# Down projections of two feed-forward layers as seven block products instead of eight

## The reference

```python
def conv_ffn(h, w_up, conv_w, conv_b, w_down):
    a, v = jnp.split(h @ w_up, 2, axis=-1)
    a = lax.conv_general_dilated(a, ...) + conv_b
    return (jax.nn.silu(a) * v) @ w_down

def swiglu(x, w_gate, w_up, w_down):
    return (jax.nn.silu(x @ w_gate) * (x @ w_up)) @ w_down
...
x = x + g2 * conv_ffn(hffn, ffn_w_up[layer], ..., ffn_w_down[layer])
...
x = x + 0.5 * swiglu(rms_norm(x, ffn1_norm[l]), ffn1_w_gate[l], ffn1_w_up[l], ffn1_w_down[l])
```

## Time and profile before

| | |
|---|---|
| Median of three runs | 2320.53 us |
| Profiled execution, its own time | 2323.76 us |
| Its span in the profile | 2322.5 us |
| TensorE (PE) busy | 2276.6 us, 98% |
| VectorE (DVE) busy | 1630.0 us, 70% |
| ScalarE (ACT) busy | 1049.5 us, 45% |
| GpSimd (POOL) busy | 667.5 us, 29% |
| Granted TensorE clock, mean | 0.996 of full |

### The profile page before, as it was taken

One profiled execution on the slowest core, in us unless ns is written; L12 is line 12 of the kernel. 1 busy time (PEld: TensorE's weight loads), 2 busy tenths in 40 slices (PEclk: granted clock), 3 DMA queues, 4 the chain that ended last, 5 costly groups with the idle time before them and its releaser, 6 DMA issues.

```text
span 2322.5 us, 33905 instructions
## 1 busy us (share of the span) xinstructions
PE 2276.6 (98%) x13709; PEld 1982.2 (85%) x13709; DVE 1630.0 (70%) x2087; ACT 1049.5 (45%) x1515; POOL 667.5 (29%) x587
## 2 busy tenths in 40 slices
PE   7999999999999999999999999999999999999999
PEld 5888977999887877777999888999888777899987
DVE  6655757988786446736988756988555984788844
ACT  4322244555333447834555445444344363544442
POOL 0111532333122028822333010333010771133200
PEclk9999999999999999999999999999999999999999
DMA  8665025776574320015775525676233212677422
GB/s 293 189 199 164 1 91 142 187 182 154 180 229 141 100 67 1 1 55 145 176 179 147 163 91 163 164 183 153 84 106 93 82 37 73 183 179 179 113 91 82
DMA packets 224083, 304.44 MB, mean 131 GB/s; under 512 B 14314, under 2 KB 165415, under 8 KB 223927
## 3 DMA queue, kind: packets, MB, share of 16 engines
q1 hardware_dynamic: 172980, 219.79, 29.3%
q0 software_dynamic: 50640, 82.29, 17.3%
q10 hardware_dynamic: 306, 0.19, 0.0%
HBM read 300.13 MB, written 2.10 MB: 130 GB/s over the span
## 4 chain that ended last, share of the span: by engine, by line
PE 82%; DVE 9%; POOL 3%; issue 2%; ACT 2%; DMA 1%; ACTq 0%; DVEq 0%; POOLq 0%
PE ps L728 45%; PE ps L1133 10%; PE ps L1135 10%; PE ps L1134 10%; DVE w_lo L2245 2%; DVE dsa_mask L2969 1%; POOL hg_k L3269 1%; PE ps L1259 1%; POOL nsa_p L3359 1%; PE ps L1275 1%; DVE small L2967 1%; DMA m_raw<-in_ada_w 1%; PE ps L700 1%; ACT w_hi L1587 1%; PE ps L669 1%
## 5 line engine op out<-in xcount | busy, mean ns | idle before, releaser
L2245 DVE TENSOR_TENSOR w_lo<-w_raw,w_hi 128x1024 fp32r<-128x1024 f32 (+1 forms) x466 | 650.1, 1396 | 506.4 <-ACT w_hi L1587 505.2
L1587 ACT ACTIVATE w_hi<-w_raw 128x1024 fp32r<-128x1024 f32 (+1 forms) x472 | 495.8, 1051 | 991.3 <-PE ps L728 647.3
L1133 PE MATMUL ps<-feat_t,w_hi 128*128 128x256 f32 x1152 | 326.5, 283 | 3.1 <-DVE hid L2667 2.2
L1134 PE MATMUL ps<-feat_t,w_hi 128*128 128x256 f32 x1152 | 326.0, 283 | 0.0
L1135 PE MATMUL ps<-feat_t,w_lo 128*128 128x256 f32 x1152 | 326.0, 283 | 0.0
L3193 POOL TENSOR_TENSOR w_raw<-w_raw,w_raw 128x1024 f32<-128x1024 f32 x72 | 178.6, 2480 | 457.2 <-DVE w_lo L2245 457.2
L728 PE MATMUL ps<-h_hi,w_hi 128*128 128x512 f32 (+1 forms) x776 | 306.1, 394 | 3.1 <-DVE w_lo L2245 1.6
L728 PE MATMUL ps<-h_hi,w_lo 128*128 128x512 f32 (+1 forms) x776 | 302.2, 389 | 0.0
L728 PE MATMUL ps<-h_lo,w_hi 128*128 128x512 f32 (+1 forms) x776 | 302.1, 389 | 0.0
L1133 PE MATMUL ps<-h_hi,w_hi 128*128 128x256 f32 x864 | 244.9, 283 | 1.9 <-DVE w_lo L2245 1.9
L728 PE MATMUL ps<-ring_hi,w_hi 128*128 128x512 f32 x616 | 242.3, 393 | 3.3 <-DVE ring_lo L2696 3.3
(11 more groups left out here) (436 smaller groups left out, 4194.7 us busy)
## 6 DMA issues: line engine op xcount, KB each, us to landing
w_raw<-in_ffn_w_up SPq DMA_DIRECT2D x126, 512.0 KB, 6.4
w_raw<-in_ffn_w_down SPq DMA_DIRECT2D x176, 256.0 KB, 3.4
w_raw<-in_ffn_w_up POOLq DMA_DIRECT2D x72, 512.0 KB, 7.5
m_raw<-in_ada_w POOLq DMA_DIRECT2D x61, 512.0 KB, 4.6
w_raw<-in_ffn_w_gate SPq DMA_DIRECT2D x54, 512.0 KB, 5.7
w_raw<-in_hg_w_in SPq DMA_DIRECT2D x64, 256.0 KB, 3.1
w_raw<-in_ffn_w_up SPq DMA_DIRECT2D x48, 256.0 KB, 3.0
w_raw<-in_nsa_w_in SPq DMA_DIRECT2D x40, 256.0 KB, 2.9
```

The source lines that it names most:

```text
L1133: K.nc.tensor.matmul(out, hi[:, w], m_hi, start=opens and kt == f == 0, stop=False, skip_group_check=True)
L1134: K.nc.tensor.matmul(out, hi[:, w], m_lo, start=False, stop=False, skip_group_check=True)
L1587: K.nc.scalar.activation(K.half(K.hi(u), width), K.half(K.raw(u), width), ACT.Copy) \
L2245: K.nc.vector.tensor_tensor(K.half(K.lo(u), width), K.half(K.raw(u), width), hi, ALU.subtract) \
```

## The change

In `ffn_b` and `ffn_c` the down projection becomes a 2 by 2 by 2 block product of seven products in the place of eight. The blocks are: even and odd inner tile of a pair `p` (11 pairs), first and second half of the outputs, and early and late 256 tokens. The matmuls have 256 columns. Their sums stay in the eight PSUM banks, in four sets of two banks, X, Y, W and V. There are two passes over the inner features: first the units `a` and `b` of all pairs (22 units of two products), then the units `c` of all pairs (11 units), then the `d` units, which hold one product of two pairs each (6 units, the last a half one). That is 39 units in the place of 22 (`DOWN_ORDER`), each split by ScalarE and VectorE as before; the weights come in seven raw buffers, and four pairs of `w_hi` and `w_lo` hold the split ones.

Sums of weight blocks: the second block of the `a` and `c` units is accumulated by a DMA that POOL issues (`gpsimd_down_add`); POOL makes two 128 by 512 additions for each `b` unit (`gpsimd_down_sums`). Sums of features: POOL makes three 128 by 256 subtractions for each pair (`gpsimd_down_feature`: t1, t3, t4), and VectorE one (`vector_down_sum`, t2). The features of a unit are 128 by 512 (`down_hi`, `down_lo`). Between the passes ScalarE copies X and W out of PSUM, and VectorE joins the sums and adds them to `xT` beside the second pass (`vector_partial`).

```diff
+            if tag in SEVEN_DOWN:
+                first, second = (slice(512 * half, 512 * half + 512) for half in halves_of(tag))
+                self.blocks[tag] = lambda kt, half: down_w[kt * P:(kt + 1) * P, (first, second)[half]]
+                block, all_of = self.blocks[tag], slice(0, 512)
+                for half in (3, 4) if halves_of(tag)[1] == 0 else (5, 6):
+                    split_held[half] = self.unit[tag, UP_GROUPS - 1, "p3"]
+                for n, (kind, p) in enumerate(DOWN_ORDER):
+                    key, slots = (tag, "down", kind, p), (0, 1, 3, 4) if halves_of(tag)[1] == 0 else (0, 1, 5, 6)
+                    u = unit(512, key, slot={DOWN_UNITS - 2: 7, DOWN_UNITS - 1: 1}.get(n, slots[n % 4]))
+                    self.unit[key] = u
+                    pieces = {"a": [(0, all_of, block(2 * p, 0)), (1, all_of, block(2 * p, 1))],
+                              "b": [(1, all_of, block(2 * p + 1, 0))],
+                              "c": [(0, all_of, block(2 * p, 0)), (1, all_of, block(2 * p + 1, 0))],
+                              "d": [(j, all_of, block(2 * (p + j) + 1, 1)) for j in range(2) if p + j < UP_GROUPS]}[kind]
+                    load(key, pieces, n % DOWN_SLOTS)
...
+SEVEN_DOWN = ("ffn_b", "ffn_c")
+DOWN_SLOTS = 7
+AFTER_HID = 60
+DOWN_ORDER = ([("a", 0)] + [(kind, p - (kind == "b")) for p in range(1, UP_GROUPS) for kind in "ab"] + [("b", UP_GROUPS - 1)] +
+              [("c", p) for p in range(UP_GROUPS)] + [("d", p) for p in range(0, UP_GROUPS, 2)])
+DOWN_UNITS = len(DOWN_ORDER)
+DOWN_AT = {key: n for n, key in enumerate(DOWN_ORDER)}
+DOWN_PRODUCTS = {"a": (("X", 0, 0), ("Y", 1, 1)), "b": (("W", 0, 1), ("V", 1, 0)), "c": (("X", 1, 1), ("W", 0, 0)), "d": (("W", 0, 0), ("W", 1, 1))}
...
+def tensor_down_tile(K, tag, n, product, j, opens=False, ends=False):
+    u, (role, w_half, m_half) = K.unit[tag, "down"] + n, product
+    hi, lo, m_hi, m_lo = K.hi(u), K.lo(u), K.down_hi[n % 4][:, m_half, :], K.down_lo[n % 4][:, m_half, :]
+    out = K.ps[:, down_bank(tag, role) + j // 2, j % 2 * 256:j % 2 * 256 + 256]
+    w = slice(512 * w_half + j * P, 512 * w_half + (j + 1) * P)
+    K.nc.tensor.matmul(out, hi[:, w], m_hi, start=opens and j % 2 == 0, stop=False, skip_group_check=True)
+    K.nc.tensor.matmul(out, hi[:, w], m_lo, start=False, stop=False, skip_group_check=True)
+    return K.nc.tensor.matmul(out, lo[:, w], m_hi, start=False, stop=ends, skip_group_check=True)
...
+    for n, (kind, p) in enumerate(DOWN_ORDER[:-2]):
+        if n == 0:
+            emptied(UP_GROUPS - 2)
+        elif (kind, p) == ("b", 0):
+            emptied(UP_GROUPS - 1)
+        elif (kind, p) == ("d", 0):
+            pe.wait_ge(*K["up_part"].at((tag, "x22")))
+        pe.wait_ge(*K["hid_low"].at((tag, n)))
+        pe.wait_ge(*K["w_low"].at(down + n))
+        products = DOWN_PRODUCTS[kind]
+        if kind == "c" and p == UP_GROUPS - 1:
+            products = products[::-1]
+        for i, product in enumerate(products):
+            if kind == "c" and p == 0:
+                pe.wait_ge(*K["first_copied"].at((tag, product[0])))
+            for j in range(4):
+                ins = tensor_down_tile(K, tag, n, product, j, kind in "ab" and p == 0, p == UP_GROUPS - 1)
+            if i == 0 and kind in "bc" and p == UP_GROUPS - 1:
+                ins.then_inc(*K["feature_sum"].up((tag, "w", kind)))
+        ins.then_inc(*K["unit_multiplied"].up(down + n))
...
+def scalar_down_high(K, tag, n):
+    act, (kind, p) = K.act, DOWN_ORDER[n]
+    if n < 4:
+        act.wait_ge(*K["unit_multiplied"].at(K.unit[tag, UP_GROUPS - 1, "p5" if n < 2 else "p6"]))
+    else:
+        act.wait_ge(*K["unit_multiplied"].at(K.unit[tag, "down"] + n - 4))
+    if kind == "b":
+        act.wait_ge(*K["feature_made"].at((tag, "down", p)))
+    else:
+        made = {"a": "t1", "c": "t3", "d": "t4"}[kind]
+        act.wait_ge(*K["pool_sum"].at((tag, "down", made, min(p + (kind == "d"), UP_GROUPS - 1))))
+    grains = 1 if (kind, p) == ("d", UP_GROUPS - 1) else 2
+    K.nc.scalar.activation(K.down_hi[n % 4][:, 0:grains, :], K.down_features(kind, p), ACT.Copy).then_inc(*K["hid_high"].up((tag, n)))
...
+def vector_down_low(K, tag, n):
+    grains = 1 if n == DOWN_UNITS - 1 else 2
+    hi = K.down_hi[n % 4][:, 0:grains, :].bitcast(F32)
+    K.dve.wait_ge(*K["hid_high"].at((tag, n)))
+    K.nc.vector.tensor_tensor(K.down_lo[n % 4][:, 0:grains, :], K.down_features(*DOWN_ORDER[n]), hi, ALU.subtract).then_inc(*K["hid_low"].up((tag, n)))
+def vector_down_sum(K, tag, p):
+    K.dve.wait_ge(*K["pool_sum"].at((tag, "down", "t1", p)))
+    K.dve.wait_ge(*K["unit_multiplied"].at(K.unit[tag, UP_GROUPS - 1, "p7" if p < 8 else "p4"]))
+    K.nc.vector.tensor_tensor(K.grains[:, AFTER_HID + p, :], K.grains[:, 4 * p + 1, :], K.grains[:, 4 * p + 3, :], ALU.add) \
+        .then_inc(*K["feature_made"].up((tag, "down", p)))
...
+    if name == "e":
+        dve.wait_ge(*K["first_copied"].at((tag, "X")))
+        vec.tensor_tensor(kept["e"], kept["x"], down_sums(K, tag, "Y"), ALU.subtract).then_inc(*K["up_part"].up((tag, "e")))
+        return
+    if name == "f":
+        dve.wait_ge(*K["up_part"].at((tag, "e")))
+        dve.wait_ge(*K["unit_multiplied"].at(K.unit[tag, "down", "b", UP_GROUPS - 1]))
+        vec.tensor_tensor(kept["f"], down_sums(K, tag, "V"), kept["e"], ALU.subtract).then_inc(*K["up_part"].up((tag, "f")))
+        return
...
+DOWN_PARTS = {22: "e", 24: "f", 26: "x22e", 28: "x21", 30: "x12f", 32: "x12", 34: "x22"}
+def vector_seven_down(K, tag, gain):
+    down, order = K.unit[tag, "down"], norm_order(tag)
+    for n in range(2, DOWN_UNITS):
+        vector_split(K, down + n)
+        vector_down_low(K, tag, n)
+        if n % 2 == 0 and n // 2 + 1 < UP_GROUPS:
+            vector_down_sum(K, tag, n // 2 + 1)
+        if tag in MOD_AMID:
+            if n % 2 and n // 2 - 1 < KD:
+                for m in mods_beside(tag, n // 2 - 1):
+                    vector_mod_unit(K, m)
+            if n == 25:
+                vector_mod_add(K, 1, MOD_AMID[tag][0], down_bank(tag, "Y"))
+        if n in DOWN_PARTS:
+            if DOWN_PARTS[n] == "x22e" and tag in MOD_AMID:
+                K.dve.wait_ge(*K["mod_ready"].at("mod1%d" % MOD_AMID[tag][0]))
+            vector_partial(K, tag, DOWN_PARTS[n], gain)
+        if n == 34:
+            for kt in order[:4]:
+                vector_add_sums(K, tag, "X", kt, gain)
+        if n >= DOWN_UNITS - 4 and tag in PLAIN:
+            vector_plain_low(K, tag, n - DOWN_UNITS + 4)
...
+def gpsimd_down_feature(K, tag, name, p):
+    g, pool = K.grains, K.pool
+    b11, b12, b21, t2 = (g[:, at, :] for at in (4 * p, 4 * p + 1, 4 * p + 2, AFTER_HID + p))
+    if name == "t1":
+        pool.wait_ge(*K["hid_gated"].at((tag, p, 1) if p < PLAIN_GROUPS else (tag, p)))
+        out, a, b = b12, b11, b12
+    elif name == "t3":
+        pool.wait_ge(*K["hid_low"].at((tag, DOWN_AT["a", p])))
+        pool.wait_ge(*K["feature_made"].at((tag, "down", p)))
+        out, a, b = b12, b11, t2
+    else:
+        pool.wait_ge(*K["hid_low"].at((tag, DOWN_AT["b", p])))
+        pool.wait_ge(*K["pool_sum"].at((tag, "down", "t3", p)))
+        out, a, b = t2, b21, t2
+    K.nc.gpsimd.tensor_tensor(out, a, b, ALU.subtract).then_inc(*K["pool_sum"].up((tag, "down", name, p)))
+def gpsimd_down_add(K, tag, i):
+    kind, p = "ac"[i // UP_GROUPS], i % UP_GROUPS
+    key, slot = (tag, "down", kind, p), K.raw_slot(K.unit[tag, "down", kind, p])
+    K.pool.wait_ge(*K.raw_landed[slot].at(key))
+    if i >= 4:
+        K.pool.wait_ge(*down_sum_landed(K, tag, "ac"[(i - 4) // UP_GROUPS], (i - 4) % UP_GROUPS))
+    half = 1 if kind == "a" else 0
+    K.nc.gpsimd.dma_start(K.w_raw[slot][:, 512 * half:512 * half + 512], K.blocks[tag](2 * p, 1) if kind == "c" else K.blocks[tag](2 * p + 1, 1),
+                          accum_op=ALU.add).then_inc(*K.sum_landed[i % 4].up(key, 16))
+def gpsimd_down_sums(K, tag, p):
+    pool = K.pool
+    a, b = (K.raw_slot(K.unit[tag, "down", kind, p]) for kind in "ab")
+    left, right = slice(0, 512), slice(512, 1024)
+    pool.wait_ge(*down_sum_landed(K, tag, "a", p))
+    pool.wait_ge(*K.raw_landed[b].at((tag, "down", "b", p)))
+    K.nc.gpsimd.tensor_tensor(K.w_raw[b][:, left], K.w_raw[a][:, left], K.w_raw[a][:, right], ALU.add).then_inc(*K["pool_sum"].up((tag, "down", "s2", p)))
+    pool.wait_ge(*K["pool_sum"].at((tag, "down", "s2", p)))
+    K.nc.gpsimd.tensor_tensor(K.w_raw[b][:, right], K.w_raw[b][:, right], K.w_raw[b][:, left], ALU.add) \
+        .then_inc(*K["pool_sum"].up((tag, "down", "s4", p)))
+def gpsimd_seven_down(K, tag):
+    for i in range(3):
+        gpsimd_down_add(K, tag, i)
+    gpsimd_down_feature(K, tag, "t1", UP_GROUPS - 2)
+    for p in range(UP_GROUPS):
+        gpsimd_down_sums(K, tag, p)
+        gpsimd_down_add(K, tag, p + 3)
+        if tag in MOD_AMID and p < KD:
+            gpsimd_mod_load(K, MODS_A + p)
+        if p == 2:
```

(9 more changed lines are left out.)

176 lines of the change are left out of this document (156 added, 20 removed).

## The result

The changed kernel takes **2379.55 us** (median of four runs, 2379.41 to 2381.32). The kernel before, run beside it, took 2321.67. The ratio is 1.0249, with a 95% interval of 1.0231 to 1.0267: 2.5% slower. I had forecast 2350 with 2324 to 2376. The direction was right, the loss twice as large as forecast, and the time 3.6 us above my range: the forecast failed, in its size. The gaps at the start of the first pass and the up projection of `ffn_c` are the terms that it had most wrong.

A forecast was written before the change was run, and what follows sets the result against it. TensorE set the pace before; after the change VectorE and POOL, unable to overlap, would. `ffn_c` +7.2 and `ffn_b` +22.3 made +29.5 us on the profiled 2323.76: 2353.3, or 2350 us for a median, range 2324 to 2376.

The forecast's parts named there:

- What bounds the kernel, and the exclusion of VectorE and POOL: Down projections: TensorE alone sets the pace before; VectorE and POOL instructions with both inputs in SBUF do not overlap.
- TensorE's gain of 9.0 us in each: Each down projection: matmuls fall from 119.9 to 110.9 us, -18.0 us in all if TensorE is kept fed.
- The rate of the first pass: VectorE plus POOL take 7.05 us a pair in `ffn_c`, 8.15 in `ffn_b` with modulation, against TensorE's 5.76: +12.9 and +21.7.
- full-duration reading: First pass: if the lock held for full durations, a pair counts 4.2 us of VectorE; total some 15 us higher, 2365.
- The start of the first pass: Third unit, split after the last group's gate, comes late: +2.9 us in `ffn_b`, +0.2 in `ffn_c`.
- I take nothing: Up projections: nine more POOL subtractions and two VectorE sums in some 180 us cost nothing to 2 us, taken as nothing.
- Second pass and `d` units: Behind the first pass: `c` units +2.1 us in `ffn_c`, +3.7 in `ffn_b`; last stretch +1 and +3; ceiling about double.
- Queued behind the gate on POOL: Start of the first pass: `ffn_b`'s modulation load and the second pair's sums wait there, counted as part of the contention.
- ScalarE and the transfers, hidden: First pass: ScalarE's splits and copies cost nothing; transfers, mainly at `c` units, add at most 4 us, 2354, within the forecast.
- sums that are free or cheap: POOL's sums run beside VectorE, 2308 us, chance 0.07; or they cost less, 2318 up to 2326, chance 0.11.
- The chain through POOL: `b` units go POOL, POOL, ScalarE, VectorE; VectorE idles in each of 20 pairs, about 1.4 us: +28, 2378 us, chance 0.13.

The follow-up runs named there:

- `tiny_all`: Changed kernel with all of POOL's new sums and subtractions cut to 8 columns, same waits, output not the reference's; 2328.19 us, 1.0014 of the kernel before.
- `tiny_t1_up`: Changed kernel with only POOL's nine t1 subtractions beside each up projection cut to 8 columns; 2370.27 us, 1.0200 of the kernel before.
- `dve_all`: Changed kernel with VectorE making all the sums that POOL made, in both projections, whole reference computed; 2333.64 us, 1.0042 of the kernel before.
- `offchain`: Changed kernel; in `ffn_b`, from the second pair, POOL's sums mostly cut to 8 columns, each followed by a full-size addition nobody awaits; 2371.79 us.

## Why the direction was right and the size wrong

- **What bounds the kernel, and the exclusion of VectorE and POOL**: right. `w_lo` took 1812 ns, `down_lo` 1100, TensorE's waits ended with `down_lo`, 46.4 of 47.5 us.
- **TensorE's gain of 9.0 us in each**: right in its pitch; where nothing was in the way, in `tiny_all`, `ffn_c` took 113.1 for 119.7, and a gap of 1.7 us at the last units was most of the rest.
- **The rate of the first pass**: right: 8.08 us a pair for 7.93 in `ffn_b`, 7.13 for 7.05 in `ffn_c` (6.85 and 6.93 in two other executions of the same first pass). In part this is luck: 7.05 was a choice between bounds of 5.98 and 7.33. The blocked instruction adds some 1.0 us, as the earlier trace rows had it. The Trainium skill, page "SBUF — State Buffer", section "Who interferes with whom", calls the lock exclusive and names the two-SBUF-input form; the traces agree on both (1812 ns for 1228 with two inputs in SBUF; 0.69 us beside POOL with one in PSUM). Its full-duration reading, which I had priced at 15 us more, is not borne out by the rate.
- **The start of the first pass**: this is the step that failed most. The term was mis-sized: 3.1 us forecast, 13.4 measured, +10.3. I priced the gaps at 2.9 and 0.2 us, from VectorE's rows of before, as if POOL stood still. The timelines of VectorE and of POOL in the changed `ffn_c`:

```profile
1677.52 1.91 DVE L2869 TENSOR_TENSOR gate_buf<-gate_buf,rstd_ffn_b 128x512 f32<-128x512 f32 x1
1679.35 2.31 DVE L2870 TENSOR_TENSOR hid<-hid,rstd_ffn_b 128x1024 f32<-128x1024 f32 x1
1681.76 2.11 DVE L2837 TENSOR_TENSOR hid<-hid,gate_buf 128x1024 f32<-128x1024 f32 x1
1683.79 2.29 DVE L2431 TENSOR_TENSOR w_lo<-w_raw,w_hi 128x1024 fp32r<-128x1024 f32 x1
```

```profile
1677.28 1.59 POOL L3536 TENSOR_TENSOR w_raw<-w_raw 128x512 f32<-128x512 f32 x1
1678.95 1.63 POOL L3538 TENSOR_TENSOR w_raw<-w_raw 128x512 f32<-128x512 f32 x1
1681.12 1.67 POOL L3536 TENSOR_TENSOR w_raw<-w_raw 128x512 f32<-128x512 f32 x1
1682.87 2.13 POOL L3538 TENSOR_TENSOR w_raw<-w_raw 128x512 f32<-128x512 f32 x1
```

  POOL sums weights for later units just while VectorE makes the last gate; four VectorE instructions in a row take 1.9 to 2.3 us, the gate's product 2.11 for 1.22. Together they take 4.3 us more than in `tiny_all`. Another 2.2 us are there before: the last part of the gate (L2866) begins 2.4 us behind the first matmul of the projection, and 0.2 us in `tiny_all`.

  In `ffn_b` it is another matter, since POOL is idle while the gate is made. Rows of VectorE and of POOL there:

```profile
1282.48 1.78 DVE L2899 TENSOR_TENSOR down_lo<-hid,down_hi 128x512 fp32r<-128x512 f32 x1
1296.11 1.94 DVE L2899 TENSOR_TENSOR down_lo<-hid,down_hi 128x512 fp32r<-128x512 f32 x1
```

```profile
1281.55 2.16 POOL L3538 TENSOR_TENSOR w_raw<-w_raw 128x512 f32<-128x512 f32 x1
1295.63 0.57 POOL L3602 DMA_DIRECT2D m_acc<-in_ada_w  x1 [7.92 <-DVE hid L2837]
```

  The first pair's weight sums, which POOL makes before the projection begins, hold up VectorE, and the last part of the gate begins 2.5 us behind the first matmul, again for 0.2 in `tiny_all`. The second pair's, which come right behind the gate, lengthen the third unit's `down_lo` by 1.3 us. With tiny sums the gaps are 3.2 and 0.3 us: my numbers, once POOL is out of the way.
- **Up projections, "I take nothing"**: failed for `ffn_c`, +7.0 us. `tiny_t1_up` shows that POOL's t1 subtractions cause it. I had read VectorE's 14.5 us of idle time from a window of `ffn_b` and did not look at `ffn_c`, where it was 10.0.
- **Second pass and `d` units**: mis-sized, +3.6 us in `ffn_b`, +2.4 in `ffn_c`, within the "about double" of the text. In `ffn_c` the stretch takes 49.4 us in `tiny_all` for 53.0 (51.6 and 52.3 in two other executions), so POOL's sums cost 2 to 4 us in it. In `ffn_b` the largest single part is the gap of 4.7 us beside POOL's squares. That its sums cost anything there is not shown: the stretch takes 61.5 us in `tiny_all`, where a transfer is late, and 57.3 in `dve_all`.
- **Queued behind the gate on POOL, "part of the contention"**, and **ScalarE and the transfers, hidden**: right for the changed kernel; TensorE's idle time ends with `down_lo` and not with them. Where the sums are cheap, in `tiny_all`, late transfers cost 5.1 us in `ffn_b`.
- **The rivals**: sums that are free or cheap are ruled out by the rates, 7.13 and 8.08 us a pair where TensorE needs 5.76. The chain through POOL gave 2378, next to the measured time, but not by its mechanism: it has VectorE idle once in each pair, and VectorE is never idle from 1296 to 1376. The 9 us of `ffn_b` that `offchain` did not bring back stay open.

The terms account for the whole: 3.7 + 6.6 at the starts, 1.5 + 0.8 in the rates, 3.6 + 2.4 behind the first passes, 7.0 in the up projection, 0.6 in the rest, and 0.2 by which the stage before is shorter in the profile than in my sum, make 26.4 us above my 29.5. The terms of the starts and of the up projection, 17.3 of the 26.4 us, missed on the same side and for one cause: I priced POOL's sums only in the loop that they belong to. Terms that share a cause do not even out, and so the range was too narrow.

## What to carry to other kernels

When work goes to an engine that excludes the bounding one, price the duration on the slower engine against every instruction of the bounding engine within reach, in the stages ahead and behind too, and not only in the loop that it belongs to. Ask for each stage how much idle time the engine has in that same stage. Where two engines exclude each other, give the work to the one that does it fastest, as in `dve_all`. A slow clock on an engine that waits for another need not be a cost: fill the gap once, and see whether the time moves and whether the low clock only went elsewhere.

## What the runs showed of the hardware that I had not expected

- A POOL operation that hardly moves data is not short beside a busy VectorE: in `tiny_all` the first 128 by 8 weight sum of a pair took 822 ns on average (the 128 by 512 one 1650), and single 128 by 8 operations in `ffn_b` took from 0.19 to 4.01 us. So the tiny sums are not quite free of load either.
- VectorE and POOL do not take turns one by one. A VectorE instruction can wait for several POOL ones that started after it. In the second pass of `ffn_c` in the changed kernel:

```profile
1770.92 4.60 DVE L2431 TENSOR_TENSOR w_lo<-w_raw,w_hi 128x1024 fp32r<-128x1024 f32 x1
```

```profile
1770.74 0.87 POOL L3525 DMA_DIRECT2D w_raw<-in_ffn_w_down  x1 [1.43 <-DMA w_raw<-in_ffn_w_down]
1771.35 3.08 POOL L3514 TENSOR_TENSOR hid<-hid 128x256 f32<-128x256 f32 x4
```

  This `w_lo` starts 0.43 us before the first of four POOL subtractions, which run back to back, and ends 1.09 us after the last of them, so it made hardly any headway before. What held it while POOL was only issuing the transfer, and why POOL kept going, is open. It differs from my reading of the earlier trace rows, by which the two take turns, and from a lock that goes to whichever starts first.
- Idle times of some microseconds were enough for the granted clock to fall: 0.60 in the 10 us window in which a gap of 6.6 us ends, 1.00 in the same window with the gap filled.
